# Reordering the products of a split-precision projection over two weight blocks, by kind, or by pairs of tiles

## The reference, cut to what matters

```
z   = rmsnorm(x) @ w_in
x  += rmsnorm(concat(A, B) @ w_out)
up  = rmsnorm(x) @ w_up                  # 1024 -> 2*2816
up  = causal_dwconv(up)
x  += rmsnorm((gelu(up[:, :2816]) * up[:, 2816:]) @ w_down)
x  += (p @ w_ple) * sigmoid(rmsnorm(x) @ w_ple_gate)
```

## Time and profile before

| what | value |
|---|---|
| median of 3 runs | 2708.77 us (2703.78 to 2709.14) |
| span of the profiled execution | 2707.0 us, 1.8 us under that median |
| PE busy | 2676.2 us, 99% of the span |
| DVE / ACT / POOL busy | 1729.9 / 921.2 / 237.0 us |
| matmul instructions on PE | 14549, of them 13080 products of `split_product` |
| mean granted clock of TensorE | 0.996 of full |

### The profile page before, as it was taken

The page is one execution under the profiler, slowest core; times in us unless marked ns, Lnnn a source line. Parts: engine busy times, 40 slices in busy tenths (PEclk is TensorE's granted clock), DMA queues, the critical chain, the costliest instruction groups (busy, mean ns, idle before and its releaser), DMA issues.

```text
span 2707.0 us, 37694 instructions
## 1 busy us (share of the span) xinstructions
PE 2676.2 (99%) x14549; PEld 2589.0 (96%) x14549; DVE 1729.9 (64%) x3699; ACT 921.2 (34%) x1932; POOL 237.0 (9%) x180
## 2 busy tenths in 40 slices
PE   9999999999999999999999999999999999999999
PEld 7989999999999999999999999999999998899998
DVE  8975898865566665555665664756866636472645
ACT  5464434453432122443321233532112425211113
POOL 4432515230000000000000000000000000000000
PEclk9999999999999999999999999999999999999999
DMA  9857989877566666565666666566666676466665
GB/s 329 318 192 272 361 333 364 324 276 297 187 230 231 231 233 232 206 253 202 230 228 235 231 226 254 193 220 227 229 233 231 213 285 145 171 240 231 233 232 203
DMA packets 125117, 660.59 MB, mean 244 GB/s; under 512 B 22010, under 2 KB 22654, under 8 KB 55182
## 3 DMA queue, kind: packets, MB, share of 16 engines
q1 hardware_dynamic: 111150, 628.29, 64.3%
q10 hardware_dynamic: 13792, 29.92, 3.4%
HBM read 533.04 MB, written 125.11 MB: 243 GB/s over the span
## 4 chain that ended last, share of the span: by engine, by line
PE 92%; DVE 4%; ACT 2%; DMA 1%; issue 1%; POOL 0%; SPq 0%; DVEq 0%; ACTq 0%; POOLq 0%
PE proj L673 29%; PE proj L674 28%; PE proj L675 28%; PE m L673 1%; PE m L674 1%; PE m L675 1%; DMA w_split<-w_kept 1%; PE m L857 1%; PE m L890 1%; PE m L891 0%; PE m L851 0%; PE m L868 0%; DMA w_raw<-in_w_units 0%; PE m L719 0%; DVE cv L1848 0%
## 5 line engine op out<-in xcount | busy, mean ns | idle before, releaser
L673 PE MATMUL proj<-h_split,w_split 128*128 128x416 f32 x2704 | 969.7, 359 | 4.1 <-DVE h_split L1782 1.9
L674 PE MATMUL proj<-h_split,w_split 128*128 128x416 f32 x2704 | 947.2, 350 | 0.0
L675 PE MATMUL proj<-h_split,w_split 128*128 128x416 f32 x2704 | 942.1, 348 | 0.0
L673 PE MATMUL proj<-f_split,w_split 128*128 128x416 f32 x1536 | 549.9, 358 | 10.3 <-POOL w_split L657 3.1
L674 PE MATMUL proj<-f_split,w_split 128*128 128x416 f32 x1536 | 539.2, 351 | 0.0
L675 PE MATMUL proj<-f_split,w_split 128*128 128x416 f32 x1536 | 536.1, 349 | 0.0
L673 PEld LDWEIGHTS proj<-h_split,w_split 128*128 128x128 f32 x2704 | 507.3, 188 | 15.3 <-issue 5.7
L675 PEld LDWEIGHTS proj<-h_split,w_split 128*128 128x128 f32 x2704 | 508.2, 188 | 9.9
L674 PEld LDWEIGHTS proj<-h_split,w_split 128*128 128x128 f32 x2704 | 508.6, 188 | 3.5 <-issue 1.4
L673 PEld LDWEIGHTS proj<-f_split,w_split 128*128 128x128 f32 x1536 | 288.9, 188 | 26.1 <-issue 6.1
L1825 DVE SCALAR_TENSOR_TENSOR cv<-a_ext,vecs,cv 128x416 f32<-128x416 f32 (+1 forms) x480 | 304.9, 684 | 0.0
(11 more groups left out here) (308 smaller groups left out, 2285.5 us busy)
## 6 DMA issues: line engine op xcount, KB each, us to landing
w_split<-w_kept SPq DMA_DIRECT2D x430, 1024.0 KB, 4.8
w_kept<-w_split SPq DMA_DIRECT2D x108, 1024.0 KB, 6.6
w_raw<-in_w_units SPq DMA_DIRECT2D x216, 256.0 KB, 4.8
x_resid<-in_x ACTq DMA_DIRECT2D x5, 1664.0 KB, 12.5
out_y<-x_resid ACTq DMA_DIRECT2D x8, 832.0 KB, 7.7
rows<-in_x ACTq DMA_DIRECT2D x4, 832.0 KB, 7.0
w_raw<-in_x ACTq DMA_DIRECT2D x3, 832.0 KB, 8.7
qkv<-in_p ACTq DMA_DIRECT2D x5, 416.0 KB, 5.3
```

The source lines that it names most:

```text
L673: mm(dst, w_hi, a_hi, start=first, stop=False)
L674: mm(dst, w_hi, a_lo, start=False, stop=False)
L675: return mm(dst, w_lo, a_hi, start=False, stop=last)
```

## The change

Three orders of products replace the order tile by tile.

- `in_turn`, used by `two_groups`: for each tile, high x high of group g, the same of group g + 1, then low weight x high activation of both, then high weight x low activation of both.
- `whole_group` with `by_kind`, used for the groups of the first half of the up-projection behind the pair: all 8 tiles high x high, then all 8 with the low weight, then all 8 with the low activation.
- `whole_group` with `in_pairs`, used for the 22 groups of the second half: the three kinds over two tiles, then the next two tiles.

The products, their number, their banks, their weight units, and the waits and signals of a group stay; in `two_groups` the waits of group g + 1 now stand behind the first product of group g and not behind its third, and the last product of group g is the last but one of the pair and not the fourth from the end.

```diff
+            def whole_group(blk, last, g, act, order):
+
+                    if not (last and g in extra):
+                        pe.wait_ge(s_evac.sem, s_evac.free(blk, g - 4 if last and g - 2 in extra else g))
+                    blocks = blocks_of(g, last)
+                    u = blocks[0][0]
+                    pe.wait_ge(s_w[u % RING].sem, s_w[u % RING].done(blk, u // RING + 1))
+                    for n, (low_w, low_a, k) in enumerate(order):
+                        ins = mm(bank_of(g, last)[:, 0:T], w[:, u % RING, low_w, k * P:(k + 1) * P], act[:, k, low_a, :],
+                                 start=n == 0, stop=n == len(order) - 1)
+                    ins.then_inc(s_proj.sem, 1)
+
+            by_kind = [(low_w, low_a, k) for low_w, low_a in ((0, 0), (1, 0), (0, 1)) for k in range(KD)]
+            in_pairs = [(low_w, low_a, k + n) for k in range(0, KD, 2) for low_w, low_a in ((0, 0), (1, 0), (0, 1)) for n in range(2)]
...
+            def in_turn(blk, last, g, act, ready, n):
+
+                    for low_w, low_a in ((0, 0), (1, 0), (0, 1)):
+                        for one in (g, g + 1):
+                            u, b = blocks_of(one, last)[n]
+                            if n == 0 and not low_w and not low_a:
+                                if not (last and one in extra):
+                                    pe.wait_ge(s_evac.sem, s_evac.free(blk, one - 4 if last and one - 2 in extra else one))
+                                pe.wait_ge(s_w[u % RING].sem, s_w[u % RING].done(blk, u // RING + 1))
+                            if one == g and not low_w and not low_a:
+                                ready(n)
+                            room = w_spare[:, :, :] if last and u in spare else w[:, u % RING, :, :]
+                            ins = mm(bank_of(one, last)[:, 0:T], room[:, low_w, b * P:b * P + P], act[:, n, low_a, :],
+                                     start=n == 0 and not low_w and not low_a, stop=n == KD - 1 and low_a == 1)
+                            if n == KD - 1 and low_a:
+                                ins.then_inc(s_proj.sem, 1)
...
                     if n < KD:
-                        group(blk, last, g, act, ready, (n, n + 1))
-                        group(blk, last, g + 1, act, None, (n, n + 1))
+                        in_turn(blk, last, g, act, ready, n)
...
                     for g in range(up + ((4 if last else 2) if half == 0 else 0), up + 2 * FH):
-                        group(blk, last, g, h)
+                        whole_group(blk, last, g, h, in_pairs if half else by_kind)
```

## The result

The changed kernel takes 2714.62 us (median of 6 runs, 2711.05 to 2717.68) where the kernel before takes 2708.64 (6 runs): a ratio of 1.0023, 95% interval 1.0013 to 1.0034, or 6.0 us more. Of the runs behind it the profiled one is among the longer, 2717.13 us with a span of 2715.3, so its trace shows 8.4 us more span than the one before, some 2 us beyond the difference of the medians.

What follows compares the result with a forecast made beforehand. It took PE, busy 99% of the span, to bound the kernel through distances between product starts. Pair waits added 6.8 us, the free distance nothing: span 2713.8, plus 1.8 for the median, gives 2715.6 us, range 2697 to 2725.

Steps and rivals of the forecast that it cites:

- The waits of a pair: At begins and ends of pairs, one product instead of three covers the bank copy: 18 x 0.38 = 6.8 us lost.
- rival E: The loss at the pairs doesn't reach the end, since PE would have waited later anyway: 2709 us, chance 0.13.
- The free distance: Time between starts of products while PE runs freely, 0.1889 us each; the new orders were taken to change it by nothing.
- the sign that the prediction had set for being wrong: Either stretch of up groups, 90.7 us in half 0 or 99.7 in half 1, shorter or longer by more than 0.5%.
- Rival B: The kind of step sets the distance between products and a repeated weight block is dear: 2702 us, chance 0.29.
- sorts of step: Transitions between products: same weights again 0.191 us, other weights with activation low to high 0.189, high to high 0.186.
- Rival C: The 0.0139 us a product above the bfloat16 distance go in all reordered products: 77 us saved, 2639 us, chance 0.03.
- Rival D: The new orders cost more in each step, up to the dearest sort, 13.8 us added: 2729 us, chance 0.10.

Runs made afterwards that it cites:

- pairs_only: Against the kernel before, only the pairs of groups go product by product, up groups stay tile by tile; ratio 1.0021 (1.0012 to 1.0031).
- turn_inside: As the changed kernel, but the first and last tile of a pair go group by group; ratio 1.0015 to the kernel before.
- stagger_by_kind: Against the kernel before, a pair's second group goes one tile behind the first (not in blk 4), all up groups by kind; 2701.25 us, ratio 0.9974.

## Why the prediction was right, point by point

**The waits of a pair** were the mechanism, at the predicted places and nearly at the predicted price. The chain of 0.95 to 0.96 us stayed, one product covers it instead of three, and 18 x 0.38 = 6.8 us came out as 6.0. It fell short in four pairs. Blk 4's gate pair took, with its third group, 15.39 us before and 15.38 after, and blk 0's gate pair 0.37 us more instead of 0.76: both had stood later on for an activation tile, and that stand took up the loss. That is rival E, in a few of 18 places. In blk 2's up pair and blk 3's gate pair the begin stands for the weights of the second group, not for the bank: there the step went from 1.04 to 1.31 us and from 0.70 to 0.87, so these two begins lost 0.27 and 0.17, not the 0.38 that the prediction took for them too. The call ahead of the blocks, the other way, lost 0.57 and not 0.38. `pairs_only` shows that the pairs alone give the loss, `turn_inside` that the first and the last tile alone give it, `stagger_by_kind` that more products ahead of the wait take the stand away.

One figure of it was wrong in the text: I gave the step behind the first product as about 0.58 us. That is the time PE stands; the step is that plus the product itself, 0.77, as I had it for the end.

**The free distance** is the step that was off. I put it at nothing, and it moved in both halves: -1.55 us by kind and +2.95 in pairs of tiles, which left +1.4. The second half became 0.59% longer, and over 0.5% was the sign that the prediction had set for being wrong: on this term it was. That the sum stayed this near is partly luck, since the two had opposite signs and the pairs came out 0.8 short; in the trace pairs and up groups make 7.4 us, the medians differ by 6.0. The formula that the prediction quotes from the Trainium skill (TensorE: Matmul & The Clock Gate, section Back-to-back issue gap) goes by columns alone, and the page gives it for an isolated matmul, not for a stream. Here the same 416 columns took 0.1878 to 0.1900 us at a granted clock of 1.00, by the order, and the measurement decides.

**Rival B** fell, though the order by kind did save 1.55 us of the 6.4 that it gave it. Its sorts of step were real but put down to the wrong operand: with no weights repeated the distance is the same to 0.02 us in 90.8, and the gaps follow the activation part. The reason given against it, that a short step is paid back in the next, held: by kind 22 of 24 steps stay with one activation part (15 high to high, 7 low to low), and they take 0.1882, not 0.186.

**Rival C** didn't occur: the surplus over the bfloat16 distance stayed in every order tried, at 0.012 to 0.014 us. **Rival D** occurred in part: the order of two tiles cost 0.0011 us a product more in the second half, not D's 0.0025, and the order by kind cost less and not more.

What stays open: why a float32r product takes 0.188 to 0.190 us where the bfloat16 one of the same columns takes 0.175, and how the entry chooses the rhythm. The runs show that the entry matters: in the second half a group by kind put ahead changed it, and the places counted above agree. By what it does so they don't show, nor why one stand of eleven left the slow rhythm.

## What to carry to other kernels

When two accumulation groups are interleaved, look at how many products lie between a group's last one and the next use of its bank: interleaving more finely makes both groups end together, and takes cover from the copy of the first. Letting one group run a tile ahead adds no product and hid the whole copy here wherever the next tiles were ready; where they weren't, in blk 0, the pair became 0.35 us longer than before. A difference of a few nanoseconds between sorts of step is not a saving until the order with only the cheap sort has been run: what one step wins the next can give back.

## What the runs showed of the hardware

The distance between float32r products isn't one number. With the same columns, banks and count of weight loads it was 0.1889 us tile by tile, 0.1882 by kind over eight or four tiles whatever the order of the tiles, and either 0.1900 or about 0.188 over two tiles, steady over 14 to 22 groups in a row, with the granted clock at 1.00 in every stretch that was looked at, of the slow rhythm and of the fast. Tile by tile the single gaps follow the part of the activation read, not the weights loaded. And the distance has a memory: over two tiles the sequence kept the rhythm that it entered with, until a stand at most.
